# ScalarE's copy of the turned probabilities ahead of the exponentials of the newest item, in the attention of a transformer block

## Chip, cores and metric

The kernel runs on one core of a Trainium2 chip. The metric is the device time of one execution in microseconds, the median of three runs. One core has five engines: TensorE (PE), VectorE (DVE), ScalarE (ACT), GpSimd (POOL) and SyncE (SP), each with its own instruction stream. They are ordered against each other by semaphores alone.

## What is computed

One block of a model with 512 tokens of 1024 values: an RWKV mixer beside a sparse attention (8 heads of 64 in 2 key groups), a gated merge, and a mixture of 32 experts. The change lies in the attention. Cut to it, the reference is:

```
s_s = einsum('bqghd,bgqnld->bghqnl', qg, k_sel) * scale
p_s = masked_softmax(s_s, mask_s)
o_s = einsum('bghqnl,bgqnld->bqghd', p_s, v_sel)
s_w = einsum('bqghd,bkgd->bghqk', qg, kwin) * scale
p_w = masked_softmax(s_w, mask_w)
o_w = einsum('bghqk,bkgd->bqghd', p_w, vwin)
o = gb[..., 0:1] * o_c + gb[..., 1:2] * o_s + gb[..., 2:3] * o_w
```

With 512 tokens there are 8 blocks of 64, and up to 16 may be selected, so the selected branch covers all earlier tokens. The window is 512 wide and covers them too. Both branches are causal attention over at most 512 keys, each with its own keys and values. The third, compressed branch (o_c) has 32 columns per query tile and head.

## The kernel before

The kernel is written by hand in stages. A stage opens its buffers, each engine gets its program in one block, and the stage ends with a barrier of all engines (`end_stage`, L173). Stage 1 projects and prepares, stage 2 is the attention (L1077 to L1309), stage 3 the RWKV scan and what follows it, and the last ones merge and run the experts. The weights come through a ring of 2 MB slots; a slot is refilled when the engines have let it go.

Stage 2 has 32 items. Item t is (j, i, b): j one of 4 head positions, i one of 4 query tiles of 128 tokens, b the branch. For both key groups g it treats query head 4g + j. Tile i has 128(i+1) keys (`rows_of`). The list `items` runs over j, within it over i in the order 3, 0, 2, 1, and within that over both branches. So a group of eight items has 512, 512, 128, 128, 384, 384, 256, 256 keys, and there are four groups. `LAG` is 3.

An item passes these steps:

- TensorE: scores of both groups into PSUM banks 0 and 1 or 2 and 3, by turns (L1251, causal mask added by L1254).
- VectorE: negated row maximum (L1173, tile `mx`).
- ScalarE: two exponentials into `prob`, with the row sums into `rsum` (L1200). There are four `prob` buffers.
- VectorE: reciprocal of the sums (L1177).
- GpSimd: scaling of `prob` by that and by the gate (L1123).
- TensorE: transposes of `prob` into PSUM banks 4 and 5 (L1267). There is only this one pair of banks for them.
- Copy of the transposes to `probT` in SBUF: VectorE for even items (L1185), ScalarE for odd ones (L1212).
- TensorE: product with the values, accumulated in bank 6 or 7 over a group (L1280).

Two more steps come in between: at round 7 the compressed probabilities are transposed (L1300) and copied by ScalarE (L1215), and at the end of each group the output of the group is completed (L1288) and copied by ScalarE (L1219).

The order on each engine is the order of the code. TensorE's program by rounds t is:

```
for t in range(NI + LAG + 1):
    if t < NI:
        scores(t)
...
    if 0 <= t - LAG < NI:
        turned(t - LAG)
    if 0 <= t - LAG - 1:
        weighted(t - LAG - 1)
```

`scores(t)` waits until the exponentials of item t-2 are done, since they read the same banks (`a_ex`). `turned(t)` waits for GpSimd's scaling of item t (`a_scl`) and for the copy of item t-1 (`a_evD` or `a_evA`). `weighted(t)` waits for the copy of item t. VectorE takes in round t the maximum of item t, the reciprocal of item t-1 and, where t-3 is even, the copy of item t-3. ScalarE takes in round t the exponentials of item t and, where t-3 is odd, the copy of item t-3. The exponentials wait for the maximum (`a_mx`) and for the transposes of item t-4 (`a_TR`), the copy for the transposes of its own item (`a_TR`) and for the product of the item two before (`a_PV`).

Of the kernel before, what the change touches and what calls it, by code (L numbers as in the profile page):

```python
# [48 lines left out]
ACT = mybir.ActivationFunctionType  # L49
# [101 lines left out]
def build(nc, A, out):  # L151
    consts_np, at, NC = constants()
    units = stream_units(A)
    index = {name: n for n, (name, _) in enumerate(units)}
    NU = len(units)
    where = [0, 2, 1, 0, 2] + [n % RP for n in range(FRONT, NU - 2)] + [RP, RP + 1]
    total, arrived, fills, turn_of = [0] * R, [], [0] * R, []
    for n, (_, parts) in enumerate(units):
        total[where[n]] += 16 * len(parts) if n >= FRONT else 0
        arrived.append(total[where[n]])  # L160
        turn_of.append(fills[where[n]])
        fills[where[n]] += 1
# [3 lines left out]
    with ExitStack() as top:  # L166
# [12 lines left out]
        def alloc(ctx, name, shape, dt=F32):  # L179
            return ctx.enter_context(nc.sbuf_tensor(name, shape, dt))  # L180
# [12 lines left out]
        ps = top.enter_context(nc.psum_tensor("ps", [P, 8, 512], F32))  # L193
# [167 lines left out]
        ztiles.insert(zg0 + 1, ("gs", None, 0, 0))  # L361
        zg_of = {n: m for m, n in enumerate(n for n, t in enumerate(ztiles) if t[0] == "zg")}
        last_of = {u: n for n, (_, u, _, _) in enumerate(ztiles) if u}


# [29 lines left out]
        with nc.Block() as block:  # L395
            @block.sync
            def _(sp):
                sp.dma_start(crow[:, :], A["c"][0].rearrange("(p k) -> p k", k=KD)).then_inc(s_c, 16)
                sp.dma_start(x, A["x"][0].rearrange("(i p) d -> p i d", p=P)).then_inc(s_h, 16)
                sp.dma_start(cst[:, 0:T], A["consts"][:, 0:T]).then_inc(s_const, 16)  # L400
                load_units(sp, 0, index["zr0"])
                sp.dma_start(cst[:, T:], A["consts"][:, T:NC]).then_inc(s_const2, 16)
                load_units(sp, index["zr0"], index["w1k"])
                sp.wait_ge(w_use, CT)
                sp.wait_ge(w_b, CT)
                sp.wait_ge(s_ze, 20)
                for parity in range(2):
                    for g in range(2):
                        sp.dma_start(kc2[HD * parity:HD * parity + HD, :, g, 0:T - parity],
                                     kcvc[HD * g:HD * g + HD, :, parity:T]).then_inc(c_kc, 16)  # L410
                load_units(sp, index["w1k"], index["w1v"] + 1)
                sp.wait_ge(s_x, 2)
                for m, rows in enumerate((inv, invT)):
                    for k in range(P // SUB):
                        r = slice(SUB * k, SUB * k + SUB)
                        sp.dma_start(inv_dram[m, r, :].rearrange("t (h c) -> h t c", c=SUB), rows[r, :, :]).then_inc(s_xst, 16)
                for n in range(2):
                    sp.wait_ge(s_gd[n], 16 * 8)
# [662 lines left out]
        probT = [alloc(stage2, f"probT{n}", [P, 2, T]) for n in range(2)]  # L1081
# [15 lines left out]
        NI = len(items)  # L1097
        GI = NI // CT
        LAG = 3

        def rows_of(t):
            return P * (items[t][1] + 1)

        with nc.Block() as block:
# [82 lines left out]
            @block.scalar  # L1187
            def _(act):
                for i in range(NT):
                    act.wait_ge(a_qT, i + 1)  # L1190
                    act.activation(qT[:, :, P * i:P * i + P], ps[:, i, :].rearrange("p (j t) -> p j t", j=CT),
                                   ACT.Copy, scale=HD ** -0.5).then_inc(a_q, 1)
                for t in range(NI + LAG + 2):
                    if t < NI:
                        act.wait_ge(a_mx, t + 1)
                        if t >= 4:
                            act.wait_ge(a_TR, t - 3)
                        n = rows_of(t)
                        for g in range(2):
                            ins = act.activation(prob[t % 4][:, g, 0:n], ps[:, 2 * (t % 2) + g, 0:n], ACT.Exp,  # L1200
                                                 bias=mx[:, t % 4, g:g + 1], accum_out=rsum[:, t % 4, g:g + 1])
                        ins.then_inc(a_ex, 1)
                    if t == 2:
                        for g in range(2):
                            act.wait_ge(a_csub, g + 1)
                            act.activation(pcs[:, g, :], pcs[:, g, :], ACT.Exp).then_inc(a_cex, 1)
                    e = t - LAG
                    if 0 <= e < NI and e % 2 == 1:
                        act.wait_ge(a_TR, e + 1)
                        if e >= 2:  # L1210
                            act.wait_ge(a_PV, e - 1)
                        act.activation(probT[e % 2][:, :, 0:rows_of(e)], ps[:, 4:6, 0:rows_of(e)], ACT.Copy).then_inc(a_evA, 1)  # L1212
                    if t == 7:
                        act.wait_ge(a_cT, 1)
                        act.activation(pcT[:, :, :], ps[:, 4:6, :], ACT.Copy).then_inc(a_cTe, 1)  # L1215
                    o = (t - LAG - 1) // GI - 1
                    if o >= 0 and (t - LAG - 1) % GI == 0:
                        act.wait_ge(a_o, o + 1)
                        act.activation(ynT[:, o, :], ps[:, 6 + o % 2, :], ACT.Copy).then_inc(a_oe, 1)  # L1219
# [1547 lines left out]
```

## Time and profile before

| what | value |
|---|---|
| median of three runs | 1197.09 us (1195.36 to 1203.29) |
| profiled execution | 1198.17 us |
| its span | 1196.4 us |
| TensorE matmul busy | 1030.1 us, 86% of the span |
| VectorE busy | 418.7 us, 35% |
| ScalarE busy | 203.8 us, 17% |
| GpSimd busy | 150.8 us, 13% |
| ScalarE copies L1212 in stage 2 | 16, 378 to 1025 ns each |
| ScalarE exponentials L1200 in stage 2 | 64, 349 to 689 ns each |
| first scores to last copy of stage 2 | 378.2 to 476.9 us |

Times in the rows are microseconds from the start of the span unless marked ns. PE is TensorE's matmul, PEld its weight load. In brackets a timeline row has the idle time of the engine just before it and what ended it. Ends of matmuls are modelled. A wait for several semaphores is put down to the one whose engine finished last in the profile, which need not be the one waited for. The granted clock (PEclk) is a share of TensorE's full speed, and DMA is the mean busy share of 16 DMA engines.

### The profile page before, as it was taken

To read this page: it belongs to the slowest core of one execution; us is meant where nothing else is said; L and a number is where in the kernel's file an instruction comes from. 1 tells how busy PE (TensorE), PEld (TensorE's weight loads), DVE (VectorE), ACT (ScalarE), POOL (GpSimd) and SP (SyncE) were. 2 spreads that over 40 slices of the span, in tenths; PEclk is the share of its full clock that TensorE was granted. 3 is DMA by queue.
4 is the path that set the end of the run, shared out by engine and by line. 5 is a ranking of instruction groups with operands and counts; after the bars stand their busy time and mean duration, and the time that the engine had idled before them with its cause. 6 is when DMAs were issued, how large, how long until landed. Compare 5 with 4: busy or idle time off the path is not lost.

```text
span 1196.4 us, 13390 instructions
## 1 busy us (share of the span) xinstructions
PE 1030.1 (86%) x5421; PEld 504.4 (42%) x5421; DVE 418.7 (35%) x736; ACT 203.8 (17%) x441; POOL 150.8 (13%) x219
## 2 busy tenths in 40 slices
PE   5999999999998888998999759898777888888776
PEld 4443344454445555776444523333322333333232
DVE  4563437463164453457423551111111111100016
ACT  4011123332003454222101200000000000000003
POOL 4100001050201343212000010000000000000000
PEclk8999999999999999999999969999999989999999
DMA  9923517323945000100772469999999999999995
GB/s 350 382 88 106 182 66 280 137 79 128 247 125 165 1 1 1 64 2 2 311 279 118 175 248 421 429 426 426 429 426 427 427 427 427 427 426 428 407 388 215
DMA packets 75760, 301.81 MB, mean 252 GB/s; under 512 B 21478, under 2 KB 27976, under 8 KB 63409
## 3 DMA queue, kind: packets, MB, share of 16 engines
q1 hardware_dynamic: 62178, 280.11, 59.3%
q0 software_dynamic: 6912, 15.59, 3.4%
q10 hardware_dynamic: 6608, 5.24, 1.5%
q8 instruction: 44, 0.72, 0.3%
q14 instruction: 18, 0.15, 0.0%
HBM read 286.03 MB, written 22.03 MB: 257 GB/s over the span
## 4 chain that ended last, share of the span: by engine, by line
PE 25%; DMA 21%; DVE 3%; issue 2%; ACT 1%; DVEq 0%; ACTq 0%; POOLq 0%
PE ps L2638 10%; DMA mg<-in_moe_w_down_dram 6%; DMA uT<-in_moe_w_gate_dram 6%; DMA ring<-in_moe_w_down_dram 5%; PE ps L2661 5%; PE ps L2579 5%; DMA ring<-in_moe_w_gate_dram 3%; PE ps L2530 3%; DMA uT<-y_dram 1%; PE ps L2621 1%; DVE zrT L2385 1%; DMA y_dram<-zrT,y_at 1%; DVE h L2438 0%; DMA zrT<-u_dram,slots 0%; DVE uT L2487 0%
## 5 line engine op out<-in xcount | busy, mean ns | idle before, releaser
L2638 PE MATMUL ps<-ring,zrT 128*64 128x512 f32 x704 | 203.0, 624 | 39.2 <-issue 17.2
L1047 PE MATMUL ps<-ring,uT 128*128 128x512 f32 x384 | 169.8, 596 | 0.6 <-PE ps L965 0.6
L2638 PEld LDWEIGHTS ps<-ring,zrT 128*64 128x64 f32 x704 | 68.7, 143 | 136.8 <-issue 136.8
L1036 PE MATMUL ps<-uT,ring 128*128 128x512 f32 x256 | 116.3, 611 | 2.0 <-DVE uT L701 1.4
L2402 DVE TENSOR_TENSOR zrT<-ps,mod 128x512 f32<-128x512 f32 x32 | 22.1, 691 | 264.9 <-PE ps L2661 264.6
L1047 PEld LDWEIGHTS ps<-ring,uT 128*128 128x128 f32 x384 | 71.4, 190 | 86.6 <-issue 86.0
L2661 PE MATMUL ps<-ring,hdT 128*64 128x512 f32 x352 | 79.9, 605 | 21.3 <-DMA ring<-in_moe_w_down_dram 18.6
L2189 ACT ACTIVATE zrT<-ps 128x512 f32<-128x512 f32 x16 | 9.6, 597 | 413.6 <-PE ps L2638 413.6
L2638 PE MATMUL ps<-uT,zrT 128*64 128x512 f32 x160 | 72.3, 605 | 7.2 <-issue 7.2
L1036 PEld LDWEIGHTS ps<-uT,ring 128*128 128x128 f32 x256 | 48.9, 195 | 66.2 <-issue 64.9
L2116 POOL DMA_INDIRECT y_dram<-zrT,y_at x15 | 15.3, 1017 | 418.5 <-DVE zrT L2402 418.5
L2393 DVE TENSOR_TENSOR zrT<-zrT,ps 128x512 f32<-128x512 f32 x16 | 11.0, 688 | 145.0 <-PE ps L2638 145.0
L2661 PEld LDWEIGHTS ps<-ring,hdT 128*64 128x64 f32 x352 | 29.4, 139 | 64.1 <-issue 64.1
L2579 PE MATMUL ps<-ring,uT 128*128 128x512 f32 x128 | 55.8, 594 | 0.0
L1123 POOL TENSOR_SCALAR prob<-prob,gate,rsum 128x512 f32<-128x512 f32 (+3 forms) x64 | 40.2, 639 | 108.4 <-DVE rsum L1177 107.5
L2661 PE MATMUL ps<-mod,hdT 128*64 128x512 f32 x80 | 37.0, 617 | 8.9 <-DMA mg<-in_moe_w_down_dram 7.2
L655 DVE SCALAR_TENSOR_TENSOR acc<-ring,csil,acc 128x512 f32<-128x512 f32 x56 | 43.0, 768 | 2.0
L2638 PE MATMUL ps<-mg,zrT 128*64 128x512 f32 x80 | 35.3, 593 | 9.6 <-DMA uT<-in_moe_w_gate_dram 6.6
L1200 ACT ACTIVATE prob<-ps,mx 128x512 f32<-128x512 f32 (+3 forms) x64 | 33.2, 523 | 43.8 <-DVE mx L1173 43.2
L1173 DVE TENSOR_REDUCE mx<-ps 128x2 f32<-128x1024 f32 (+3 forms) x32 | 26.4, 824 | 36.3 <-PE ps L1254 36.1
L2638 PE MATMUL ps<-mod,zrT 128*64 128x512 f32 x80 | 38.7, 641 | 0.0
L2661 PE MATMUL ps<-mg,hdT 128*64 128x512 f32 x80 | 37.1, 619 | 0.0
(428 smaller groups left out, 1287.7 us busy)
## 6 DMA issues: line engine op xcount, KB each, us to landing
ring<-in_moe_w_gate_dram SPq DMA_DIRECT2D x22, 2048.0 KB, 33.3
ring<-in_moe_w_up_dram SPq DMA_DIRECT2D x20, 2048.0 KB, 33.8
ring<-in_moe_w_down_dram SPq DMA_DIRECT2D x18, 2048.0 KB, 34.2
ring<-in_w_in_dram SPq DMA_DIRECT2D x8, 2048.0 KB, 12.4
ring<-in_w_ada_dram SPq DMA_DIRECT2D x8, 2048.0 KB, 8.7
mod<-in_moe_w_down_dram SPq DMA_DIRECT2D x5, 2048.0 KB, 38.8
mg<-in_moe_w_down_dram SPq DMA_DIRECT2D x5, 2048.0 KB, 34.1
uT<-in_moe_w_up_dram SPq DMA_DIRECT2D x5, 2048.0 KB, 38.7
```

Of the source, the lines that this page charges most:

```text
L655: link(dve.scalar_tensor_tensor(a, w[:, k, :], csil[:, k:k + 1], a, ALU.mult, ALU.add))
L1036: ins = pe.matmul(ps[:, n % 4, :], slot(name, KD, w)[:, k, c0:c0 + P], uT[:, k, :], start=(k == 0), stop=(k == KD - 1))
L1047: ins = pe.matmul(ps[:, n % 4, :], uT[:, k, P * i:P * i + P], w, start=(k == 0), stop=(k == KD - 1))
L1123: ins = pool.tensor_scalar(p_, p_, gate[:, i, h3:h3 + 1], rsum[:, t % 4, g:g + 1], ALU.mult, ALU.mult)
L1173: dve.tensor_reduce(mx[:, t % 4, :], ps[:, 2 * (t % 2):2 * (t % 2) + 2, 0:rows_of(t)], AX, ALU.max, negate=True).then_inc(a_mx, 1)
L1200: ins = act.activation(prob[t % 4][:, g, 0:n], ps[:, 2 * (t % 2) + g, 0:n], ACT.Exp, bias=mx[:, t % 4, g:g + 1], accum_out=rsum[:, t % 4, ...
L2116: pool.indirect_dma_start(y_dram, bass.IndirectOffsetOnAxis(ap=y_at[:, b:b + 1], axis=0), yo[:, b % 2, :], None, bounds_check=2 * T - 1, o ...
L2402: dve.tensor_tensor(yo[:, b % 2, 512 * c:512 * c + 512], ps[:, 2 + c, :], mod[:, 5, 512 * c:512 * c + 512], ALU.mult).then_inc(e_y, 1)
L2530: ins = pe.matmul(ps[:, 2 * (n % 2) + b, :], yT[:, k, P * i:P * i + P], w[:, k, 512 * j:512 * j + 512], start=(k == 0), stop=(k == 3))
L2579: ins = pe.matmul(ps[:, 4 + n % 3, :], mgT[:, k, P * i:P * i + P], slot(f"wo{k // 4}", 4, D)[:, k % 4, 512 * j:512 * j + 512], start=(k == ...
L2638: ins = pe.matmul(ps[HALF * r:HALF * r + HALF, "gu".index(kind), :], xgT[:, b % 2, k, HALF * r:HALF * r + HALF], w[r][:, k, :], start=(k = ...
L2661: ins = pe.matmul(ps[HALF * r:HALF * r + HALF, 2 + c, :], hdT[:, j, HALF * r:HALF * r + HALF], w[r][:, j, 512 * c:512 * c + 512], start=(j ...
```

## The change

In ScalarE's loop over the rounds, the copy of the odd item t-3 is written ahead of the exponentials of item t. The waits, shapes, buffers and the other engines' programs are the same. The copy's line number becomes L1199 and that of the exponentials L1206.

```
                 for t in range(NI + LAG + 2):
+                    e = t - LAG
+                    if 0 <= e < NI and e % 2 == 1:
+                        act.wait_ge(a_TR, e + 1)
+                        if e >= 2:
+                            act.wait_ge(a_PV, e - 1)
+                        act.activation(probT[e % 2][:, :, 0:rows_of(e)], ps[:, 4:6, 0:rows_of(e)], ACT.Copy).then_inc(a_evA, 1)
                     if t < NI:
                         act.wait_ge(a_mx, t + 1)
...
                             act.activation(pcs[:, g, :], pcs[:, g, :], ACT.Exp).then_inc(a_cex, 1)
-                    e = t - LAG
-                    if 0 <= e < NI and e % 2 == 1:
-                        act.wait_ge(a_TR, e + 1)
-                        if e >= 2:
-                            act.wait_ge(a_PV, e - 1)
-                        act.activation(probT[e % 2][:, :, 0:rows_of(e)], ps[:, 4:6, 0:rows_of(e)], ACT.Copy).then_inc(a_evA, 1)
                     if t == 7:
```

ScalarE, a group of the attention before, from the first exponential of item 17 (`prob1`) to those of item 22 (`prob2`); `probT1` is the copy, `ring` the output of a group:

```order
L1200 ACTIVATE prob1,rsum<-ps,mx 128x512 x2
L1200 ACTIVATE prob2,rsum<-ps,mx 128x128 x2
L1212 ACTIVATE probT1<-ps 128x2x256
L1200 ACTIVATE prob3,rsum<-ps,mx 128x128 x2
L1200 ACTIVATE prob0,rsum<-ps,mx 128x384 x2
L1212 ACTIVATE probT1<-ps 128x1024
L1219 ACTIVATE ring<-ps 128x512
L1200 ACTIVATE prob1,rsum<-ps,mx 128x384 x2
L1200 ACTIVATE prob2,rsum<-ps,mx 128x256 x2
```

The same place on ScalarE in the changed kernel:

```order
L1206 ACTIVATE prob1,rsum<-ps,mx 128x512 x2
L1199 ACTIVATE probT1<-ps 128x2x256
L1206 ACTIVATE prob2,rsum<-ps,mx 128x128 x2
L1206 ACTIVATE prob3,rsum<-ps,mx 128x128 x2
L1199 ACTIVATE probT1<-ps 128x1024
L1206 ACTIVATE prob0,rsum<-ps,mx 128x384 x2
L1219 ACTIVATE ring<-ps 128x512
L1206 ACTIVATE prob1,rsum<-ps,mx 128x384 x2
L1199 ACTIVATE probT1<-ps 128x2x128
L1206 ACTIVATE prob2,rsum<-ps,mx 128x256 x2
```

Each copy has moved up past one pair of exponentials, that of the even item of its round.

ScalarE at the end of the attention before, from the exponentials of item 30 (`prob2`) on:

```order
L1200 ACTIVATE prob2,rsum<-ps,mx 128x256 x2
L1212 ACTIVATE probT1<-ps 128x2x128
L1200 ACTIVATE prob3,rsum<-ps,mx 128x256 x2
L1212 ACTIVATE probT1<-ps 128x2x384
L1212 ACTIVATE probT1<-ps 128x2x256
L1219 ACTIVATE ring<-ps 128x512
```

And in the changed kernel:

```order
L1199 ACTIVATE probT1<-ps 128x2x128
L1206 ACTIVATE prob2,rsum<-ps,mx 128x256 x2
L1206 ACTIVATE prob3,rsum<-ps,mx 128x256 x2
L1199 ACTIVATE probT1<-ps 128x2x384
L1199 ACTIVATE probT1<-ps 128x2x256
L1219 ACTIVATE ring<-ps 128x512
```

The last two copies have no exponentials beside them in their rounds and stand where they stood.

## Rows read from the trace of the kernel before

**Rows 1.** Waits, 370 to 480 us: total us, times, longest
```profile
PE ps L1267 <- ACT probT L1212: 4.4, 9, 0.8
PE ps L1267 <- POOL prob L1123: 2.3, 3, 0.8
```
**Rows 2.** Stretches: length, busy PE, PEld, DVE, ACT, POOL; PEclk, DMA share, GB/s
```profile
404.00:424.50 20.50, 18.27 (x170) 11.45 (x168) 9.64 (x20) 11.89 (x37) 9.50 (x16) 1.00 0.01 2
468.00:472.00 4.00, 3.39 (x21) 2.76 (x22) 0.54 (x2) 0.81 (x1) 1.09 (x2) 0.59 0.00 0
475.00:575.00 100.00, 90.81 (x1394) 66.79 (x1390) 55.58 (x102) 24.90 (x53) 23.19 (x37) 0.97 0.07 22
700.00:1155.00 455.00, 369.35 (x1684) 150.64 (x1684) 55.13 (x77) 18.19 (x32) 29.71 (x30) 0.96 0.99 414
```
**Rows 3.** Timeline of the second group: start, us, engine, line, out<-in, count [idle before]
```profile
403.98 0.29 PE L1254 MATMUL ps<-causal_bf,ident_bf 128*128 128x128 bf16 x2
404.10 0.82 PE L1267 MATMUL ps<-cst,prob 128*128 128x128 f32 x6
...
406.90 0.81 ACT L1212 ACTIVATE probT<-ps 128x768 f32<-128x768 f32 x1
407.04 1.23 DVE L1173 TENSOR_REDUCE mx<-ps 128x2 f32<-128x1024 f32 x1 [1.45 <-PE ps L1254]
...
407.85 0.63 PE L1267 MATMUL ps<-cst,prob 128*128 128x128 f32 x4 [0.85 <-ACT probT L1212]
...
408.52 0.69 DVE L1185 COPY probT<-ps 128x512 f32<-128x512 f32 x1 [0.18 <-PE ps L1267]
...
409.76 0.61 PE L1267 MATMUL ps<-cst,prob 128*128 128x128 f32 x4
...
411.12 0.59 ACT L1212 ACTIVATE probT<-ps 128x512 f32<-128x512 f32 x1
...
411.86 1.06 PE L1267 MATMUL ps<-cst,prob 128*128 128x128 f32 x8 [0.27 <-ACT probT L1212]
...
415.42 1.04 PE L1267 MATMUL ps<-cst,prob 128*128 128x128 f32 x8
...
416.61 0.58 ACT L1200 ACTIVATE prob<-ps,mx 128x384 f32<-128x384 f32 x1 [3.71 <-DVE mx L1173]
...
417.74 1.02 ACT L1212 ACTIVATE probT<-ps 128x1024 f32<-128x1024 f32 x1
...
418.90 0.41 PE L1267 MATMUL ps<-cst,prob 128*128 128x128 f32 x2 [0.36 <-ACT probT L1212]
...
419.58 0.58 ACT L1200 ACTIVATE prob<-ps,mx 128x384 f32<-128x384 f32 x1 [0.33 <-DVE mx L1173]
419.71 1.31 POOL L1123 TENSOR_SCALAR prob<-prob,gate,rsum 128x384 f32<-128x384 f32 x2 [2.08 <-DVE rsum L1177]
...
420.26 0.70 PE L1251 MATMUL ps<-kT,qT 64*128 64x256 f32 x4
...
421.02 0.39 PE L1267 MATMUL ps<-cst,prob 128*128 128x128 f32 x2
...
421.71 0.70 PE L1251 MATMUL ps<-kT,qT 64*128 64x256 f32 x4
...
422.87 0.38 ACT L1212 ACTIVATE probT<-ps 128x256 f32<-128x256 f32 x1
...
423.39 0.84 PE L1267 MATMUL ps<-cst,prob 128*128 128x128 f32 x6 [0.76 <-POOL prob L1123]
```
**Rows 4.** Timeline of the first group, TensorE behind ScalarE's L1215
```profile
401.74 0.87 PE L1267 MATMUL ps<-cst,prob 128*128 128x128 f32 x6 [1.11 <-ACT early L1215]
```
**Rows 5.** Timeline of the end of the attention, TensorE's transposes of items 28 and 29
```profile
466.63 0.84 PE L1267 MATMUL ps<-cst,prob 128*128 128x128 f32 x6 [0.76 <-POOL prob L1123]
...
468.61 1.42 PE L1267 MATMUL ps<-cst,prob 128*128 128x128 f32 x6 [0.77 <-DVE probT L1185]
```
**Rows 6.** Timeline of SyncE, the first issue of expert weights
```profile
612.46 0.81 SPq L1974 DMA_DIRECT2D ring<-in_moe_w_gate_dram x2
```

## Prediction

> **What bounds the kernel now.** I read the table of waits of the attention stage first, then the table by stretches, then the timeline of one group of eight items, then the end of the stage.
>
> The waits [rows 1] show TensorE held before its transposes of the probabilities (L1267). It waits 9 times, 4.4 us in total, for ScalarE's copy L1212, and 3 times, 2.3 us, by name for GpSimd's scaling L1123. No engine is full in this stage: in 404 to 424.5 us TensorE is busy 18.27 of 20.50 us and ScalarE 11.89 [rows 2]. TensorE's own work is thus the bound, broken by short stops, and each stop costs span. After the stage the DMA share is 0.07 in 475 to 575 us and 0.99 in 700 to 1155 us [rows 2]: the kernel's last part goes by the weight stream.
>
> The timeline shows how a stop arises [rows 3]. Call S the scores of an item, TR its transposes, PV its product with the values. TensorE's round t is S(t), TR(t-3), PV(t-4). TR(5) ends at 404.10 + 0.82 = 404.92 us, so its result could be copied from then on. ScalarE first takes the two exponentials of item 8, and the copy starts only at 406.90 and ends at 407.71. TR(6), whose PSUM banks are those of the copy, starts at 407.85 after 0.85 us of idle TensorE. The same happens with the copies at 411.12 (0.27 us idle), 417.74 (0.36) and 422.87 (0.76). The row at 423.39 names GpSimd as releaser of the last, but this TR is item 12's, and GpSimd had finished item 12 at 419.71 + 1.31 = 421.02. ScalarE's copy ended at 422.87 + 0.38 = 423.25, 0.14 before TR, the same distance as 407.71 to 407.85. I put this stop down to ScalarE as well; the GpSimd instruction that ended then scales item 13. So all 12 stops of these two rows of [rows 1], 6.7 us, are ScalarE's: three groups of 0.85 + 0.27 + 0.36 + 0.76 = 2.24 us.
>
> **The change part by part.** Nothing is added or removed: ScalarE keeps 64 exponentials and 16 copies of the same shapes. Each copy moves ahead of the two exponentials of its round. It waits, as before, for TR of its item (and a PV that precedes that TR on TensorE). No DMA is moved, and no queue but ScalarE's.
>
> I replay one group, items 8 to 15, by its rows. A TR that waits for nothing starts before the matmul ahead of it is through: S(8)'s last piece ends at 403.98 + 0.29 = 404.27, TR(5) starts at 404.10, 0.17 earlier [rows 3]. A removed stop is thus worth its idle time and about 0.15 us more: 2.24 + 4 x 0.15 = 2.84 us, if nothing else is late.
>
> What is late next, stop by stop:
> - TR(6): the copy runs 404.96 to 405.77 instead of 406.90 to 407.71. TR(6) gains 0.85 + 0.15 = 1.00.
> - TR(7) needs VectorE's copy of item 6. TR(6) now ends at 408.48 - 1.00 = 407.48, but VectorE is in the maximum of item 9 until 407.04 + 1.23 = 408.27 [rows 3]. Its copy (0.69) ends at about 409.0, and TR(7) starts at 409.13 instead of 409.76. Of the 1.00 us, 0.63 is left: 0.37 turns into a wait for VectorE.
> - TR(8): copy 7 starts after TR(7), 409.78, ends at 410.37; TensorE comes at 411.86 - 0.63 - 0.27 - 0.15 = 410.81. Gain so far 1.05.
> - TR(10): TR(9) ends at 415.42 + 1.04 - 1.05 = 415.41, the copy of 1.02 at 416.47; TensorE comes at 418.90 - 1.05 - 0.52 = 417.33. Gain so far 1.57.
> - TR(12): TR(11) ends at 421.02 + 0.39 - 1.57 = 419.84, the copy of 0.38 at 420.26; TensorE comes at 423.39 - 1.57 - 0.92 = 420.90. GpSimd's part of item 12, moved with the maximum by about 1, ends near 420.1. Gain 2.49 us a group.
>
> What the exponentials pay: S(t+2) waits for the exponentials of t. Those of item 12 would be free to start at 416.61 - 1.05 = 415.56 but stand behind the copy until 416.37, 0.81 late. The two take about 1.24 (0.58 each and the reading of a sum) and end at 417.61; S(14) comes at 420.26 - 1.57 = 418.69, a slack of 1.08. Those of item 13 start at about 418.53, are done at 419.77, and S(15) comes at 421.71 - 1.57 = 420.14: 0.37 less about 0.1 of signal, the tightest place. The four exponentials behind a copy are late by 0.1, 0.8, 0.8 and 0. All of it lies beside TensorE's work, so I cost it at nothing. If the cover were gone, it is 1.8 us a group.
>
> Groups: items 8 to 15, 16 to 23 and 24 to 31 show the same four stops. In the last group the end is different: TR(29) waits for VectorE's copy of item 28 [rows 5], which must first finish the earlier moved maximum of item 31; I find 2.36 instead of 2.49. The first group gains little. Its one stop by a copy, that of item 3, stands before another wait: TensorE next waits 1.11 us for ScalarE's L1215 [rows 4], which comes behind the exponentials of item 7 in both orders. ScalarE goes from them to L1215 without idling, so only about 0.2 us is gained. After item 31 no exponential is left, and a copy such as that after TR(29) waits for TR in both orders. Sum: 2 x 2.49 + 2.36 + 0.2 = 7.5 us.
>
> Bounds: above, the overlap is kept and VectorE costs nothing, 3 x 2.84 + 0.2 = 8.7 us. Below, the 1.8 us a group of the exponentials counts in full, 7.5 - 5.4 = 2.1 us. I take 7.5, since each slack above is positive, if small.
>
> The stage ends in a barrier of all engines, so its end moves as a whole. The expert weights are first issued at 612.46 us [rows 6], long after, on releases by engines behind the barrier. I carry the gain to the end undiminished. The profiled execution took 1198.17 us for a span of 1196.4; minus 7.5 is 1190.7. Its median of three runs is 1.1 us lower, which gives 1189.6; I say 1190.0.
>
> On the clock, 468 to 472 us has a granted clock of 0.59 [rows 2], so partly at the lower of the two levels, 1.2 GHz, after a stretch in which TensorE stood 0.76 us before TR(28), TR(12)'s counterpart, and 0.77 us before TR(29) [rows 5]. Six transposes took 1.42 us there against 0.84 at full clock [rows 3]. At full clock up to 4 x (1 - 0.59) = 1.6 us would be saved. The Trainium skill, "TensorE: Matmul & The Clock Gate", section "What's actually happening", says that the slow state is the default and activity releases it; by that a denser stage could keep 2.4 GHz here and the sum would be 9.1. By the row alone, one of the two stops before the fall stays, so I leave it out of the sum and let the range hold it.
>
> **The rivals.**
> 1. The name in the wait table is right: GpSimd holds TR(12) and its two counterparts. Then 3 x 0.92 = 2.8 us stays and the gain is 4.7: 1192.4. For it speaks the table of waits, against it the end of GpSimd's item 12 at 421.02.
> 2. The stage stays at full clock at its end, and the VectorE wait is smaller: gain 9 to 10 us, 1187.5.
> 3. The weight stream takes it back: the last part has the DMA engines busy 0.99, and if its start were set by something other than the stage, the time would be 1197. Against it: there are nearly no transfers in 475 to 575 us, and the first weights are issued at 612.
> 4. Slower: ScalarE does its work in order, so a copy that waits for TR(t-3) holds the exponentials, and with them the maximum, reciprocal, scaling and S(t+2). The place is the even rounds. Late by 1.8 us a group, plus about 2 us at item 4, where transposes run at 1.2 GHz, this is 7.4 us if none of it is hidden, and if at the same time TensorE's stops are not the copies' but those of the chain of exponentials: 1198.17 + 7.4 - 1.1 = 1204.5. It decides as soon as the delay is above the slack of S(t+2), 0.3 us at item 15 and 1.1 at item 14. The stop rows name the copy and not L1200, which speaks against it. The Trainium skill says in "TensorE: Matmul & The Clock Gate", section "Architectural detail: the array is 16× 32×32, not 1× 128×128", that ScalarE's queue is strict FIFO; no rule there lets an exponential pass the waiting copy, and the order of starts on ScalarE in the trace agrees.
>
> **How the numbers follow.** The forecast gets 0.62, rival 1 gets 0.12, rival 2 gets 0.13, rival 3 gets 0.09, rival 4 gets 0.04. A measurement of this kernel tells about 1%, 12 us, from no change: its three runs lie 7.9 us apart. The forecast alone has 1187.5 to 1192.5. The range takes in rivals 1 and 2 and the runs' own scatter: 1186.0 to 1195.5. Faster by over 1% needs a time below 1185.1, which only rival 2 with some scatter reaches: 0.06. Slower by over 1% is beyond rival 4's sum: 0.02. Within 1%: 0.92.
>
> **What would show it.** After: the rows L1267 behind ScalarE's copy and behind GpSimd both gone or below 1 us in total; a new wait of TR(7), TR(15) and TR(23) for VectorE's copy of about 0.4 us; a group of eight in 19.1 us instead of 21.6; the barrier at the stage's end 7.5 us earlier, and the first weight issue near 605. Wrong would be: S waiting for exponentials by more than 1 us in total, the GpSimd row unchanged at 2.3 us, or a stage 7 us shorter with an unchanged end.

## The result and the profile after

The changed kernel takes 1189.44 us (median of 6 runs, 1185.54 to 1190.57), the kernel before 1198.91 us (6 runs, 1195.36 to 1203.29). The ratio is 0.9914, with a 95% interval of 0.9886 to 0.9943: 0.9% less time, beyond the scatter of the runs. The profiled execution took 1189.59 us for a span of 1187.8 us, against 1196.4 us before: 8.6 us less. A later job with 6 runs of the changed kernel and 11 of the one before gave 0.9902 (0.9878 to 0.9926).

The waits of TensorE in the two steady groups, 404 to 446 us, in the changed kernel (total us, times, longest):

```profile
PE ps L1267 <- DVE probT L1185: 0.4, 2, 0.2
```

That is the only row of TensorE's matmuls in this stretch. The rows that name ScalarE's copy and GpSimd, 4.4 and 2.3 us over the whole attention in [rows 1], are both gone here; before, they held 2.9 and 1.5 us of the same 42 us. The stretches answer to [rows 2], with the same columns:

```profile
404.00:424.50 20.50, 20.32 (x184) 12.27 (x181) 11.21 (x21) 11.97 (x37) 9.38 (x16) 1.00 0.01 2
475.00:575.00 100.00, 92.08 (x1385) 64.97 (x1382) 56.59 (x105) 25.08 (x53) 21.02 (x34) 1.00 0.13 49
700.00:1155.00 455.00, 374.89 (x1681) 150.25 (x1677) 51.16 (x65) 18.20 (x32) 28.42 (x28) 0.96 1.00 419
```

TensorE is busy 20.32 of 20.50 us now, against 18.27: in the steady groups hardly any idle time of TensorE is left to remove. The timeline of the second group answers to [rows 3]. S(8) starts at 404.64 here, 1.73 us later than before:

```profile
405.83 0.82 PE L1267 MATMUL ps<-cst,prob 128*128 128x128 f32 x6
...
406.69 0.81 ACT L1199 ACTIVATE probT<-ps 128x768 f32<-128x768 f32 x1 [3.27 <-PE ps L1267]
...
408.57 0.61 PE L1267 MATMUL ps<-cst,prob 128*128 128x128 f32 x4
408.77 1.23 DVE L1173 TENSOR_REDUCE mx<-ps 128x2 f32<-128x1024 f32 x1 [1.45 <-PE ps L1254]
...
409.98 0.67 DVE L1185 COPY probT<-ps 128x512 f32<-128x512 f32 x1
...
410.80 0.63 PE L1267 MATMUL ps<-cst,prob 128*128 128x128 f32 x4 [0.18 <-DVE probT L1185]
...
412.49 1.04 PE L1267 MATMUL ps<-cst,prob 128*128 128x128 f32 x8
...
417.11 1.03 ACT L1199 ACTIVATE probT<-ps 128x1024 f32<-128x1024 f32 x1 [3.15 <-PE ps L1267]
418.03 0.92 PE L1251 MATMUL ps<-kT,qT 64*128 64x384 f32 x4
418.03 0.57 ACT L1206 ACTIVATE prob<-ps,mx 128x384 f32<-128x384 f32 x1
...
420.34 0.70 PE L1251 MATMUL ps<-kT,qT 64*128 64x256 f32 x4
...
421.79 0.70 PE L1251 MATMUL ps<-kT,qT 64*128 64x256 f32 x4
...
422.54 0.83 PE L1267 MATMUL ps<-cst,prob 128*128 128x128 f32 x6
```

ScalarE now stands idle until TR(5) is through and copies at once (406.69). TR(6), TR(8) and TR(12), at 408.57, 412.49 and 422.54, have no idle time before them. TR(7) at 410.80 has 0.18 us, behind VectorE's copy: the new wait is where it was forecast, and its idle time is half of the 0.4 us named there. The exponentials of item 12 start behind the copy at 418.03 without idle time, and S(14) comes at 420.34 without waiting. The group, S(8) to S(16), takes 19.03 us instead of 21.62.

The first group and the end of the stage answer to [rows 4] and [rows 5], SyncE's first issue of expert weights to [rows 6]:

```profile
403.47 0.77 PE L1267 MATMUL ps<-cst,prob 128*128 128x128 f32 x5 [1.87 <-ACT early L1215]
...
462.56 0.85 PE L1267 MATMUL ps<-cst,prob 128*128 128x128 f32 x6 [0.77 <-DVE probT L1185]
...
603.53 0.80 SPq L1974 DMA_DIRECT2D ring<-in_moe_w_gate_dram x2
```

TensorE waits 1.87 us for L1215, where it waited 1.11: the stop of 0.76 us at item 3 has only moved there. TR(29) takes 0.85 us, not 1.42, and the granted clock is 1.00 from S(31) to the end of the stage. The first weights are issued 8.9 us earlier, and the end follows: the stream of weights takes nothing back.

By traces, mark to mark: "attention" is from SyncE's transfer `mod_dram<-mod` to the first one behind the barrier, `xd<-inv_dram`, "RWKV stage" from there to the first `ring<-gates_dram`.

| us | S(8) to S(16) | S(16) to S(24) | attention | RWKV stage |
|---|---|---|---|---|
| before, three executions | 21.62, 21.61, 21.62 | 21.62, 21.61, 21.62 | 104.71, 105.27, 106.37 | 94.79, 94.41, 94.80 |
| changed, three executions | 19.03, 19.01, 19.03 | 19.02, 19.02, 19.02 | 97.60, 97.19, 97.53 | 93.25, 93.23, 93.35 |
| e2 | 20.68 | 20.68 | 102.45 | 91.65 |
| e3 | 19.96 | 19.96 | 100.53 | 97.85 |
| e4 | 20.71 | 19.95 | 99.01 | 93.01 |
| e5 | 20.00 | 19.37 | 100.03 | 93.25 |
| e6 | 21.79 | 22.80 | 109.14 | 91.55 |
| e7 | 19.03 | 19.02 | 96.37 | 91.66 |
| e8 | 19.03 | 19.02 | 96.37 | 97.64 |
| e12 | 19.02 | 19.02 | 95.83 | 91.55 |

### The profile page after: what moved, and what is told of

Read it like the earlier page. It is cut to its first block, busy times and chain, and to the rows that moved or that the text cites. A ratio compares the mean times of both kernels' runs of the same rounds, so it can differ in the third digit from the quotient of the medians.

```text
span 1187.8 us, 13390 instructions
## 1 busy us (share of the span) xinstructions
PE 1032.5 (87%) x5421; PEld 503.8 (42%) x5421; DVE 418.4 (35%) x736; ACT 204.0 (17%) x441; POOL 150.4 (13%) x219
## 4 chain that ended last, share of the span: by engine, by line
PE 25%; DMA 21%; DVE 3%; issue 2%; ACT 1%; DVEq 0%; ACTq 0%; POOLq 0%
PE ps L2638 11%; DMA ring<-in_moe_w_down_dram 9%; DMA ring<-in_moe_w_gate_dram 8%; PE ps L2661 5%; PE ps L2579 5%; PE ps L2530 3%; DMA uT<-in_moe_w_gate_dram 3%; DMA uT<-y_dram 1%; DMA y_dram<-zrT,y_at 1%; PE ps L2546 1%; PE ps L2621 1%; DVE zrT L2385 1%; DVE h L2438 0%; DMA zrT<-u_dram,slots 0%; DVE uT L2487 0%
## 5 line engine op out<-in xcount | busy, mean ns | idle before, releaser
L1047 PEld LDWEIGHTS ps<-ring,uT 128*128 128x128 f32 x384 | 71.4, 190 | 86.5 <-issue 86.0
L2579 PEld LDWEIGHTS ps<-ring,uT 128*128 128x128 f32 x128 | 24.0, 190 | 28.7 <-issue 28.7
```

The source lines that it names most:

```text
L1047: ins = pe.matmul(ps[:, n % 4, :], uT[:, k, P * i:P * i + P], w, start=(k == 0), stop=(k == KD - 1))
L2579: ins = pe.matmul(ps[:, 4 + n % 3, :], mgT[:, k, P * i:P * i + P], slot(f"wo{k // 4}", 4, D)[:, k % 4, 512 * j:512 * j + 512], start=(k == ...
```

## The experiments

**e1, the changed kernel again.** No edit.

> The changed kernel itself once more, to see what of its trace belongs to one execution. Theory: the steady groups of eight items (first scores of item 8 to first scores of item 16, and on to item 24) are set by the order of ScalarE and come out at 19.0 us again, while the start of the stage and the level of the granted clock there belong to the execution and may move by 1 to 2 us. Rival: the groups' length itself varies by more than 0.2 us between executions, and the 19.03 us against 21.62 us of the kernel before is partly chance.

Groups of 19.01 and 19.02 us, total 1188.95 us. The group's length is a property of the order, good to 0.02 us; the rival falls. So the experiments below are read by the groups, which tell 0.1 us apart, and not by the total, which tells some us.

**e2, only the copies of items 3, 11, 19 and 27 ahead.** In the changed kernel:

```
-                    if 0 <= e < NI and e % 2 == 1:
+                    if 0 <= e < NI and e % 2 == 1 and e % 8 == 3:
...
+                    if 0 <= e < NI and e % 2 == 1 and not (e % 8 == 3):
```

the second loop body standing behind the exponentials, as before.

> Only the copies of items 3, 11, 19 and 27 stand ahead of the exponentials, the other twelve behind, as before. The stop behind item 11 is the one that the profile puts down to GpSimd. Theory (it is ScalarE's copy): TensorE's stop of 0.76 us before the transposes of item 12 goes and the group is 21.62 - 0.92 = 20.7 us. Rival (GpSimd holds it, as named): the stop of 0.76 us and the group of 21.6 us stay.

The timeline of e2 around TR(12):

```profile
419.68 0.41 PE L1273 MATMUL ps<-cst,prob 128*128 128x128 f32 x2 [0.35 <-ACT probT L1218]
...
422.22 0.38 ACT L1199 ACTIVATE probT<-ps 128x256 f32<-128x256 f32 x1 [0.63 <-PE ps L1273]
...
423.24 0.83 PE L1273 MATMUL ps<-cst,prob 128*128 128x128 f32 x6
```

The copies left behind still cost their stops (0.35 before TR(10)). TR(12) at 423.24, which the profile of before had waiting for GpSimd, has no idle time, although GpSimd's program is as it was. The group is 20.68 us, 0.94 less than 21.62. The stop was ScalarE's copy, and the name in the wait row was wrong. That the gain is 0.94 for an idle time of 0.76 us puts the overlap of a TR that waits for nothing at 0.18 us. The total was 1192.37 us.

**e3, all copies ahead but those four.** The condition of e2 the other way round, `e % 8 != 3`.

> All copies stand ahead of the exponentials but those of items 3, 11, 19 and 27. Theory: the stop of 0.76 us before the transposes of item 12 is back, the group is 19.03 + 0.92 = 19.95 us. Rival (GpSimd holds it and comes earlier by itself when the other stops go): the group stays at 19.0 to 19.2 us.

```profile
422.65 2.54 POOL L1123 TENSOR_SCALAR prob<-prob,gate,rsum 128x384 f32<-128x384 f32 x4 [0.53 <-DVE rsum L1177]
...
423.42 0.38 ACT L1218 ACTIVATE probT<-ps 128x256 f32<-128x256 f32 x1
423.95 0.85 PE L1273 MATMUL ps<-cst,prob 128*128 128x128 f32 x6 [0.76 <-POOL prob L1123]
```

The stop of 0.76 us is back, again under GpSimd's name, and 423.42 + 0.38 = 423.80 is the copy's end, 0.15 before TR(12). GpSimd's own row begins with item 13 and is not needed by it. The groups are 19.96 us as forecast (19.95). e2 and e3 add up: 0.94 and 1.66 make 2.60 us, the change's 2.59. The total of e3 is 1197.79 us all the same, because its RWKV stage took 97.85 us (below).

**e4, the same move on VectorE.** In the changed kernel, VectorE's copy of the even item is put ahead of the maximum, except in round 7:

```
                 for t in range(NI + LAG):
+                    e = t - LAG
+                    if e >= 0 and e % 2 == 0 and t != 7:
+                        dve.wait_ge(a_TR, e + 1)
+                        if e >= 2:
+                            dve.wait_ge(a_PV, e - 1)
+                        dve.tensor_copy(probT[e % 2][:, :, 0:rows_of(e)], ps[:, 4:6, 0:rows_of(e)]).then_inc(a_evD, 1)
```

> The same move on VectorE: its copy of the even item t-3 ahead of the maximum of item t, except in round 7. Theory (a copy moved ahead is free only where the work behind it does not feed the next scores soon): here the maximum starts 0.6 to 2 us later, and with it the exponentials, so scores wait for exponentials at two or three places in a group and the group gets longer, to about 20.5 us (20.0 to 22), although the stop of 0.18 us before the transposes of item 7 goes. Rival (the earlier the copy the better): the group is 18.85 us.

The timeline of e4:

```profile
405.73 0.69 DVE L1174 COPY probT<-ps 128x512 f32<-128x512 f32 x1 [1.89 <-PE ps L1273]
406.34 1.21 DVE L1179 TENSOR_REDUCE mx<-ps 128x2 f32<-128x1024 f32 x1
...
407.58 0.69 ACT L1212 ACTIVATE prob<-ps,mx 128x512 f32<-128x512 f32 x1 [2.23 <-DVE mx L1179]
...
409.08 0.49 PE L1257 MATMUL ps<-kT,qT 64*128 64x128 f32 x4 [0.91 <-ACT prob L1212]
```

VectorE stood idle 1.89 us for TR(6) with the maximum of item 9 behind the waiting copy. ScalarE then waited for it, and S(11) waited 0.91 us for the exponentials of item 9; S(15) waited 0.18. TR(7) has no stop any more. The steady group is 19.95 us, 0.93 longer than the changed kernel's and just below the expected range of 20.0 to 22 (the first, 20.71, still begins at half clock). So the same move loses on the engine whose later work feeds the next scores at once. The total, 1189.6 us, does not show it.

**e5 and e6, one and two idle copies ahead of the exponentials.** They probe how much delay is free. In e5, behind the moved copy:

```
+                    if t >= 10 and t % 2 == 0 and t < NI:
+                        act.activation(pcs[:, :, :], pcT[:, :, :], ACT.Copy)
```

In e6 the same copy stands there twice, the second waiting for the first.

> The changed kernel with one extra ScalarE copy of 128x1024 (about 1.0 us, into a buffer no longer used) between the moved copy and the exponentials, in the even rounds from 10 on. It asks how much delay of the exponentials is free. Theory (slack of S(14) about 1.1 us and of S(15) 0.3 us behind the exponentials): nearly all of it is hidden, the group grows by 0 to 0.5 us from 19.03 us, though four copies of 1.0 us are added. Rival (the exponentials are already the bound): the group grows by 2 us or more.

> As e5, with two such copies one behind the other (about 2.0 us). Theory: above the slack the delay shows: scores wait for exponentials at items 10, 14 and 15, and the group grows by 2 to 4 us, to 21 to 23 us, as long as that of the kernel before. Rival (ScalarE has room, as its 12 of 20.5 busy us say): the group grows by less than 1 us.

The exponentials of item 12, S(14) and S(16), first in e5, then in e6:

```profile
419.87 0.57 ACT L1208 ACTIVATE prob<-ps,mx 128x384 f32<-128x384 f32 x1
...
421.23 0.70 PE L1253 MATMUL ps<-kT,qT 64*128 64x256 f32 x4
...
424.89 1.13 PE L1253 MATMUL ps<-kT,qT 64*128 64x512 f32 x4 [0.18 <-ACT prob L1208]
```

```profile
418.73 0.56 ACT L1211 ACTIVATE prob<-ps,mx 128x384 f32<-128x384 f32 x1
...
420.00 0.70 PE L1256 MATMUL ps<-kT,qT 64*128 64x256 f32 x4 [0.93 <-ACT prob L1211]
...
424.83 1.13 PE L1256 MATMUL ps<-kT,qT 64*128 64x512 f32 x4 [1.26 <-ACT prob L1211]
```

With one extra microsecond S(14) still comes without idle time, S(16) waits 0.18 us, and the steady group grows by only 0.35 us (19.37; the first, 20.00, begins at half clock, as in e4). With two it grows by 3.78 us (22.80), and S(14), S(16) and S(18) wait 0.93, 1.26 and 0.94 us; S(15), where a wait was expected, waits only 0.10. The totals were 1191.02 and 1198.40 us.

How much delay is free can be read from e6 and e5. In e6 the exponentials of item 12 came 2.04 us late (418.73 is 2.04 behind S(13) at 416.69; in the changed kernel both start at 418.03). S(14) came 3.31 us behind S(13), in the changed kernel 2.31. So it paid 1.00, and 1.04 us were free, where 1.08 was forecast. The tighter place is S(16). In e5 the exponentials of item 14 started 1.03 us behind S(15), in the changed kernel 0.23, so they were 0.80 late, and S(16) paid 0.25 of it (2.13 us behind S(15) instead of 1.88): 0.55 us were free.

The steady group of e6 is 1.19 us longer than that of the kernel before. What the old order takes with the same extra copies was not run, so these two runs give the slack of the new order and not the point at which it loses against the old one. In every even round the exponentials start behind the copies, never ahead of them. The Trainium skill, "TensorE: Matmul & The Clock Gate", section "Architectural detail: the array is 16× 32×32, not 1× 128×128", calls ScalarE strict FIFO, and the order of starts in e6 agrees.

**e7, the compressed copy ahead too.** L1215's three lines are moved from behind the exponentials of round 7 to behind the moved copy.

> The changed kernel with one more move: in round 7 the copy of the compressed probabilities stands ahead of the exponentials of item 7 as well. In the changed kernel TensorE waits 1.87 us for it. Theory: it starts when the transposes end, at about 401.6 us in that trace instead of 402.39, so the wait shrinks by 0.8 us to about 1.1 us, and the rest of the stage comes 0.8 us earlier. Rival: the delayed exponentials of item 7 hold something else, and the stage's end does not move.

```profile
401.55 1.02 ACT L1202 ACTIVATE early<-ps 128x1024 f32<-128x1024 f32 x1 [0.57 <-PE ps L1300]
...
402.63 0.87 PE L1267 MATMUL ps<-cst,prob 128*128 128x128 f32 x6 [1.11 <-ACT early L1202]
```

The wait is 1.11 us instead of 1.87, and S(0) to S(8) 23.53 us instead of 24.29 at the same opening: 0.76 us, as forecast. The total was 1187.62 us.

**e8, the last four copies shared by two engines.** For items from 28 on VectorE copies key group 0 and ScalarE key group 1, and `evicted` waits for both:

```
-                        act.activation(probT[e % 2][:, :, 0:rows_of(e)], ps[:, 4:6, 0:rows_of(e)], ACT.Copy).then_inc(a_evA, 1)
+                        gs = slice(0, 2) if e < SP0 else slice(1, 2)
+                        act.activation(probT[e % 2][:, gs, 0:rows_of(e)], ps[:, 4 + gs.start:6, 0:rows_of(e)], ACT.Copy).then_inc(a_evA, 1)
```

> The changed kernel with the copies of the last four items (28 to 31) shared: VectorE takes key group 0, ScalarE key group 1. In the stage's end each transpose waits for a whole copy (0.94, 0.81, 0.69, 0.60 us). Theory: the first scores of item 31 to the last copy of the stage shrinks by 0.8 to 1.5 us from 459.83 to 469.52 us = 9.69 us. Rival: two semaphores and the start-up of each instruction eat it, change below 0.3 us.

```profile
460.48 0.49 ACT L1202 ACTIVATE probT<-ps 128x384 f32<-128x384 f32 x1 [0.36 <-PE ps L1274]
460.49 0.54 DVE L1187 COPY probT<-ps 128x384 f32<-128x384 f32 x1
461.13 0.84 PE L1274 MATMUL ps<-cst,prob 128*128 128x128 f32 x6 [0.33 <-DVE probT L1187]
```

A copy of 0.94 us became two of half the size side by side (0.49 and 0.54 us), and TR(29) waits 0.33 us instead of 0.77. From S(31) to the first transfer of the next stage it is 10.22 us instead of 11.13, 0.91 less. Yet the total was 1192.45 us, 3 us above the changed kernel. By stages, the attention is 1.1 us shorter than the changed kernel's 97.4 and the RWKV stage, with the same program, took 97.64 us, 4.4 longer.

**e9 and e10, the kernel before twice more.** No edit.

> The kernel before once more, for its trace. Theory: the groups of eight are 21.62 us again; the low clock at the end of its attention (0.59 in 468 to 472 us) and the length of the RWKV stage behind the barrier belong to the execution, so from the first scores of item 31 to the first transfer of the next stage it is about 12.1 us here (what the run with the fourth items behind has at full clock) or 13.4 us again. Rival: the low clock there comes from the kernel's order and is 13.4 us each time, so that the change gained 1.3 us by the clock.

> A third trace of the kernel before, with the same two readings: 12.1 or 13.4 us at the end of the attention, and the stretch from the first transfer of the RWKV stage to the first transfer of the merge, 94.79 us in the first trace and 93.25 us in the changed kernel. Theory: that stretch lies anywhere from 91.6 to 97.9 us, as in the eight runs so far, and the 1.5 us that it gave in the first comparison is chance. Rival: it is 94.8 us or more whenever the kernel is the one before.

The end of the attention in e9:

```profile
467.51 0.85 PE L1267 MATMUL ps<-cst,prob 128*128 128x128 f32 x6 [0.76 <-POOL prob L1123]
...
469.50 0.84 PE L1267 MATMUL ps<-cst,prob 128*128 128x128 f32 x6 [0.77 <-DVE probT L1185]
```

The stops are those of [rows 5], but TR(29) takes 0.84 us, not 1.42. From S(31) to the next stage e9 took 12.06 us and e10 13.40, as the first trace. So the order of the kernel before does not force the fall of the clock there: it came in two executions of three of that kernel, in none of the changed kernel's three, and in e6 (granted clock 0.88 from S(31) to the next stage). Whether the order makes it likelier, three against three do not show.

For the RWKV stage neither theory nor rival holds. It does not scatter over 91.6 to 97.9 us from one execution of a kernel to the next: it is 94.4 to 94.8 in three executions of before and 93.2 to 93.4 in three of the changed kernel, 1.4 us apart on average. Nor is it always 94.8 or more with the old order (94.41 in e9). Whole RWKV stages of before, the changed kernel and e12, then the stretch of 20 us of e3 that lies 60 us into it (columns as in [rows 2]):

```profile
478.35:573.14 94.79, 87.73 (x1368) 64.84 (x1368) 55.58 (x102) 23.15 (x49) 23.09 (x36) 0.96 0.07 22
```

```profile
470.96:564.21 93.25, 86.18 (x1368) 63.16 (x1368) 55.49 (x102) 23.02 (x49) 23.05 (x36) 0.98 0.07 22
```

```profile
469.26:560.81 91.55, 84.51 (x1368) 61.99 (x1368) 55.33 (x102) 23.02 (x49) 23.05 (x36) 1.00 0.07 22
```

```profile
534.26:554.26 20.00, 18.14 (x285) 16.43 (x283) 11.19 (x23) 4.94 (x10) 2.84 (x2) 0.74 0.01 2
```

The instruction counts are equal, 1368, and the mean granted clock goes 0.96, 0.98, 1.00 with 94.79, 93.25, 91.55 us. The shortest stages are those at full clock throughout, and e3 has 0.74 for 20 us in its 97.85.

The first 20 us of the stage and the 20 us that lie 60 us into it, in the first trace of before and then in e9:

```profile
478.35:498.35 20.00, 19.95 (x264) 13.97 (x264) 9.41 (x16) 3.44 (x8) 7.49 (x16) 0.91 0.28 94
...
538.35:558.35 20.00, 18.20 (x365) 16.45 (x364) 14.04 (x27) 6.16 (x12) 3.40 (x3) 0.91 0.01 2
```

```profile
477.89:497.89 20.00, 19.94 (x254) 13.64 (x255) 8.61 (x15) 3.44 (x8) 7.47 (x16) 0.86 0.28 94
...
537.89:557.89 20.00, 18.12 (x392) 16.45 (x392) 15.43 (x30) 6.04 (x12) 3.79 (x3) 1.00 0.01 2
```

The first trace and e10 have two falls of the clock, at the start and 60 us in (0.91 and 0.91). e9 comes to nearly the same length by one longer fall at the start (0.86 and 1.00). The changed kernel has the fall at the start alone (0.91 to 0.92, then 1.00), e12 has none. So the alike lengths of the kernel before come about in two ways, and its 1.4 us more are a sum of falls of the clock and no fixed price of its order.

**e11 and e12, timed in five rounds.** e11 is the changed kernel, e12 has the edits of e7 and e8 together.

> The changed kernel, timed in five rounds beside the kernel before and beside e12. Theory: the attention stage (first transfer to first transfer of the next stage) is 7.1 to 7.5 us shorter than before, and the ratio comes out at 0.993 to 0.994; the first measured ratio, 0.9914, held 1 to 2 us of chance. Rival: the whole 10 us are real, ratio 0.991 again.

> The changed kernel with the moves of e7 (compressed copy ahead in round 7) and e8 (last four copies shared by VectorE and ScalarE) together. Theory: 0.8 and 0.9 us add up, the attention stage is 1.7 us shorter than that of the changed kernel, about 95.7 us, and the median 1 to 3 us below e11's. Rival: the two do not add up or the clock takes them back, median as e11's.

| | median, us | range | ratio to before |
|---|---|---|---|
| before, 11 runs | 1202.43 | 1195.83 to 1204.57 | |
| e11, 6 runs | 1189.51 | 1189.09 to 1190.92 | 0.9902 (0.9878 to 0.9926) |
| e12, 5 runs | 1186.52 | 1184.42 to 1189.83 | 0.9876 (0.9847 to 0.9905) |

For e11 the rival was right: a ratio near 0.991 came again, and the expected 0.993 to 0.994 lies outside the interval. The attention stage was 7.9 us shorter than before on average (97.53 against 105.45), not 7.1 to 7.5. For e12 the two moves add up, 97.53 - 95.83 = 1.70 us of attention. Its median is 3.0 us below e11's. In the two traces the RWKV stage, at full clock in e12, is 1.8 us of the difference. e12 is faster than the kernel before. Against the changed kernel four of its five runs lie below all six of e11 and the fifth, 1189.83 us, among them, so that the 3.0 us are likely and not certain.

## Why the prediction was right

The time, 1189.4 us for 1190.0, was inside the range, and the account by steps holds in its main part. That the two lie only 0.6 us apart is luck: the forecast started from 1197.09 us, the median of three runs, where six gave 1198.91, and took off 7.1 us, where the medians differ by 9.5. The two errors nearly cancel.

- **The stops are ScalarE's, the one under GpSimd's name too.** Shown by e2 (stop gone, group 0.94 shorter) and e3 (stop back, 0.94 longer). Rival 1 falls.
- **A group gains 2.49 us.** Measured 2.59, alike in all executions. The overlap added to each removed stop was taken as 0.15 and is 0.17 to 0.18, and VectorE's new wait cost 0.18 us idle plus that overlap, about 0.35, where 0.37 was forecast.
- **The exponentials' delay is hidden.** Shown by the absence of any wait for them in the steady groups, and its limit by e5 and e6: 1.04 us more would be free at S(14), but only 0.55 at S(16). The prediction called S(15) the tightest place. Its exponentials do end closest to their scores (0.36 us), but they stand behind no copy, and S(16) was not looked at. The four delays that the prediction lists add up to 1.7 us a group, not 1.8, which moves only its lower bound. So rival 4 is a real mechanism that the change stays about half a microsecond short of; e4 shows it at work on VectorE.
- **The first group gains 0.2 us.** From the first scores of item 7 to TR(4) it was 3.86 us and is 403.47 - 399.80 = 3.67.
- **The last group gains 2.36 us.** This was undersized. S(24) to S(31) fell from 18.80 to 17.14 us, and from S(31) to the next stage, at full clock, from 12.06 (e9) to 11.13. The sum is 1.66 + 0.93 = 2.59. The forecast had VectorE's copy of item 28 held 0.13 us by the maximum of item 31. It starts at 461.47 us, 0.05 behind the end of TR(28), as before, so that delay did not come.
- **It is carried to the end undiminished.** Shown, so rival 3 falls: attention 105.45 us on average before and 97.44 after, 8.0 less, and from `ring<-gates_dram` to the end 623.2 to 624.5 us in three traces before and 623.6 to 624.2 in three after.

The sum of 7.5 was short of the medians' difference, 9.5 us and in the later job 12.9, and the term mainly at fault is the clock, which the sum left out. Over three traces each, the spans fell by 10.0 us. By parts: attention 8.0, of which 7.8 are three groups of 2.59 and 0.9 the low clock at its end in two of three executions of before, less 0.7 for a slower opening up to S(8). The RWKV stage gave 1.4, by its clock, and 0.9 lies ahead of the attention, which the change does not touch; what comes after the RWKV stage took 0.2 more. Rival 2 named the low clock at the attention's end; no rival named the 1.4. At full clock that end took 1.34 us less (13.40 to 12.06), where up to 1.6 was estimated. That a denser stage keeps the clock full there, which was to make the sum 9.1, is not shown: e9 kept it with the old order. The traces explain 10.0 us and not 12.9: the three traced executions of before took 1198.17 to 1201.63 us, below the later job's median of 1202.43, and what the slower runs of before (up to 1204.57) spend their time on stands in no trace.

What stays open is why the clock falls in the RWKV stage at the places it does, with one order and not with the next. The stage's starts, 469.07 us with 97.64 and 469.26 with 91.55, do not order it. No run here shifts the stage alone.

## What to carry to other kernels

Two kinds of work on one in-order engine should stand in the order in which their consumers run dry: here the copy released TensorE at once and the exponentials two rounds later, so the copy goes first, as long as its delay to the others stays below their slack. Find that slack before moving anything, at each place where the delayed work is awaited, since the same move on VectorE cost 0.93 us a group. And where a wait row names an engine that had finished what the waiter needs, look for another instruction that ended 0.1 us before the start.

## What was not expected of the hardware

From one order of the attention to another the length of the next stage, whose program no edit touched, differed by up to 6.3 us, and its granted clock with it: 91.55 us at 1.00, 97.85 us at 0.93. e3 and e8 have attention stages shorter than the kernel before by 4.9 and 9.1 us, and give 3 us of it back in the RWKV stage. Each of them was traced once, so that the edit, and not the execution, made it so is not shown for them. The Trainium skill, "TensorE: Matmul & The Clock Gate", section "What's actually happening", says that the chip's look at activity runs free of the kernel's start, so that the same kernel differs between executions. At the end of the attention this case agrees that executions differ (TR(29) 1.42 us in one execution of the kernel before and 0.84 in another). In the RWKV stage the lengths differ less, by no more than 0.4 us within three executions of each of two kernels, though in the kernel before the falls of the clock behind them are not the same ones.
